# A two-layer encoder trunk on one core: constants kept across stages, loads moved into the delta mixer, three input sets and a divided softmax division in the window attention

## The reference

```
h = x * (1 + scale) + shift                      # scale, shift, gate from a conditioning vector
x = layer_norm(alpha * x + (1 + gate) * sublayer(h))
```

```
ya = (group_norm(y_fwd + y_bwd) * gn_g + gn_b + bonus * v) * (sigmoid(z_g) @ g_up)
yb = o * rsqrt(mean(o * o) + eps) * norm_g * silu(out_gate)
mixed = concat(ya, yb) @ ab_w_out
```

```
s = q @ k.T * scale + band;  m = max(max(s), sink);  p = exp(s - m)
p = p / (sum(p) + exp(sink - m));  out = p @ v
```

## Time and profile before

| what | value |
|---|---|
| median of three runs | 3577.85 us (3577.48 to 3582.41) |
| the profiled execution, its own time | 3570.47 us |
| its span (first to last instruction) | 3568.6 us |
| TensorE busy (PE) | 3123.8 us, 88% of the span |
| VectorE busy (DVE) | 1954.1 us, 55% |
| ScalarE busy (ACT) | 1243.9 us, 35% |
| GpSimd busy (POOL) | 592.1 us, 17% |
| mean granted TensorE clock | 0.912 of full speed |

### The profile page before, as it was taken

One profiled execution on the slowest core, in us unless ns is written; L12 is line 12 of the kernel. 1 busy time (PEld: TensorE's weight loads), 2 busy tenths in 40 slices (PEclk: granted clock), 3 DMA queues, 4 the chain that ended last, 5 costly groups with the idle time before them and its releaser, 6 DMA issues. The chain is left out here.

```text
span 3568.6 us, 43985 instructions
## 1 busy us (share of the span) xinstructions
PE 3123.8 (88%) x15824; PEld 1899.2 (53%) x15824; DVE 1954.1 (55%) x4102; ACT 1243.9 (35%) x2994; POOL 592.1 (17%) x547
## 2 busy tenths in 40 slices
PE   8999999679999996995895999969967889699994
PEld 4555555357777785885454444434433445444441
DVE  3886685399889873995776000045445534500016
ACT  1112222245455543673662222222245623122213
POOL 0000100111111101121000110011057810010005
PEclk9999999779788876998896999989989999699997
DMA  8453234511111002243533999943224332499986
GB/s 268 160 177 131 63 100 140 189 33 39 39 39 36 29 28 79 87 151 115 165 129 114 361 406 377 364 146 132 80 90 139 118 124 101 148 391 367 368 302 219
DMA packets 360906, 584.04 MB, mean 164 GB/s; under 512 B 50374, under 2 KB 255846, under 8 KB 360458
## 3 DMA queue, kind: packets, MB, share of 16 engines
q1 hardware_dynamic: 287624, 346.99, 29.3%
q0 software_dynamic: 34560, 123.47, 9.7%
q10 hardware_dynamic: 38532, 111.10, 8.0%
HBM read 456.81 MB, written 124.68 MB: 163 GB/s over the span
## 5 line engine op out<-in xcount | busy, mean ns | idle before, releaser
L364 PE MATMUL inp__bank<-inp__hT,inp__w 128*128 128x512 f32 (+1 forms) x1536 | 557.9, 522 | 1.0 <-DVE inp__hT L508 1.0
L2697 PE MATMUL moe__bank<-kept__weights,moe__xT 128*128 128x512 f32 x1024 | 456.8, 599 | 10.9 <-DMA kept__weights<-in_moe_w_up_dram 6.6
L364 PEld LDWEIGHTS inp__bank<-inp__hT,inp__w 128*128 128x128 f32 x1536 | 288.6, 190 | 253.2 <-issue 239.2
L2697 PEld LDWEIGHTS moe__bank<-kept__weights,moe__xT 128*128 128x128 f32 x1024 | 191.0, 192 | 234.3 <-issue 232.5
L2143 PE MATMUL close__bank<-kept__weights,kept__catT 128*128 128x512 f32 x640 | 286.5, 602 | 18.7 <-ACT kept__catT L2248 7.5
L2815 DVE TENSOR_TENSOR moe__hid<-moe__sg,moe__bank 128x256 f32<-128x256 f32 x64 | 26.9, 421 | 478.6 <-ACT moe__sg L2758 478.6
L2714 PE MATMUL moe__bank<-moe__wdn,moe__hidT 128*128 128x512 f32 x512 | 230.5, 593 | 2.9 <-ACT moe__hidT L2762 2.9
L3491 POOL TENSOR_SCALAR attn__p<-attn__p,attn__rec 128x384 f32<-128x384 f32 x160 | 195.8, 1246 | 116.7 <-DVE attn__rec L3466 116.6
L3112 PE MATMUL cq__bank<-kept__w_in,cq__hT 128*128 128x512 f32 x480 | 211.0, 596 | 2.9 <-DVE cq__hT L3248 2.9
L2143 PEld LDWEIGHTS close__bank<-kept__weights,kept__catT 128*128 128x128 f32 x640 | 121.5, 194 | 165.5 <-issue 147.0
L433 ACT ACTIVATE inp__z<-inp__bank 128x512 f32<-128x512 f32 (+1 forms) x96 | 50.5, 526 | 403.1 <-PE inp__bank L364 403.1
(11 more groups left out here) (468 smaller groups left out, 5792.3 us busy)
## 6 DMA issues: line engine op xcount, KB each, us to landing
kept__weights<-in_moe_w_gate_dram SPq DMA_DIRECT2D x64, 1024.0 KB, 8.0
kept__weights<-in_moe_w_up_dram SPq DMA_DIRECT2D x64, 1024.0 KB, 14.7
moe__wdn<-in_moe_w_down_dram ACTq DMA_DIRECT2D x64, 1024.0 KB, 8.0
inp__wv<-in_ada_w_dram SPq DMA_DIRECT2D x10, 4096.0 KB, 16.0
scratch_y_rows<-moe__y ACTq DMA_DIRECT2D x64, 512.0 KB, 8.5
scratch_zt<-inp__tb SPq DMA_DIRECT2D x32, 640.0 KB, 5.0
inp__w<-in_ab_w_in_dram POOLq DMA_DIRECT2D x31, 512.0 KB, 4.8
rwkv__rk<-scratch_zt SPq DMA_DIRECT2D x20, 512.0 KB, 3.9
```

The source lines that it names most:

```text
L364: mm = pe.matmul(zbank[j][g][:, 0:n], w[:, j, k, :], hT[:, k, t0:t0 + n], start=k == 0, stop=k == KC - 1)
L2697: mm = pe.matmul(bank[2 + j][:], xT[:, j, k, :], wgu[:, j, k].rearrange("p a n -> p (a n)"), start=k == 0, stop=k == KC - 1)
```

## The change

One copy of the first 629 constant columns, the router's three tensors and the sink row is kept in SBUF from the delta mixer on; the phases behind it no longer load their own. In `const_f`, `unit` and `eye4` move behind the masks, so that `delta` loads 704 columns (352 KB) beside the kept copy (314.5 KB). SP issues the closing part's loads inside the delta mixer's loop: five after the store of step 3, two in each of steps 4 to 6. In `close0` the first wait is for four loads in place of six, and `v`, `og` and `gn` are waited for in `joined`. In the last stage there are four sets of diagonals, three built at the start, the others ahead of each tile's squares. In the attention there are three input sets, loaded two tiles ahead, and the second head's division of every odd pair goes from GpSimd to VectorE: 40 of 160.

```diff
@@ constants
-                  ("unit", 256), ("eye4", 16)] + [
+                  ] + [
...
+        ... + [("unit", 256), ("eye4", 16), ("incl", P), ...
@@ deltanet_mixer
-        first = CONST["ident"].start
+        first = CONST["unit"].start
@@ sync
                 sp.dma_start(cf[:], a["const_f"][:, first:CONST_W]).then_inc(cst, 16)
-                sp.dma_start(ones[:], a["const_f"][:, CONST["ones"]]).then_inc(cst, 16)
+                sp.dma_start(a["cf"][:], a["const_f"][:, 0:CONST["ident"].stop]).then_inc(a["cf_l"], 16)
...
+                def closing_consts():      # gup, ng (cst_l); rw, rb, tok (router_l): five loads
...
+                def closing_heads(i):      # bon, glow of tile i (heads_l[i]): two loads
...
                     if have(s):
                         store_o(s)
+                    if s == 3:
+                        closing_consts()
+                    if 3 < s < 7:
+                        closing_heads(s - 4)
@@ close_mixer, sync
-                if layer:
-                    sp.dma_start(cf[:], a["const_f"][:, 0:CONST["ident"].stop]).then_inc(cst, 16)
...
-                        sp.dma_start(v[:, r], ...).then_inc(heads_l[r], 16)
-                        sp.dma_start(og[:, r], ...).then_inc(heads_l[r], 16)
-                        sp.dma_start(glow[:, r], ...).then_inc(heads_l[r], 16)
+                        if i > 2:          # bon and glow
...
+                        sp.dma_start(v[:, r], ...).then_inc(late_l[r], 16)
+                        sp.dma_start(og[:, r], ...).then_inc(late_l[r], 16)
...
-                sp.dma_start(rw[:], ...)   # and rb, tok
@@ close_mixer, vector
-                    dve.wait_ge(heads_l[r], 96 * (i // 3) + 96)
+                    dve.wait_ge(heads_l[r], 64 * (i // 3) + 64)
...
+                    dve.wait_ge(late_l[r], 32 * (i // 3) + 32)
+                    if i == 0:
+                        dve.wait_ge(gn_l, 32)
@@ experts, gpsimd
-                        pool.dma_start(a["ident"][:], a["const_f"][:, CONST["ident"]]).then_inc(a["cols_l"], 16)
+                        pool.dma_start(a["sink"][:], a["at_sink"].broadcast_to([P, AT_H])).then_inc(a["cols_l"], 16)
@@ combine, scalar
-                diagonals(0)
-                diagonals(1)
+                for i in range(3):
+                    diagonals(i)
                 for i in range(NT):
+                    if i + 3 < NT:
+                        diagonals(i + 3)
                     squares(i)
                     norm_rows(i)
-                    if i + 2 < NT:
-                        diagonals(i + 2)
@@ window_attention
-        v = ph.sb("v", [P, 2, 3, VW])
+        v = ph.sb("v", [P, 3, 3, VW])      # qT, kT and band alike
...
+        def on_vector(t, e):
+            return e == 1 and t % 2 == 1
...
                 load(0)
-                sp.dma_start(sink[:], a["at_sink"].broadcast_to([P, AT_H])).then_inc(cst, 16)
-                sp.dma_start(ident[:], a["const_f"][:, CONST["ident"]]).then_inc(cst, 16)
                 load(1)
+                load(2)
...
-                    if 0 < i < TILES - 1:
-                        load(i + 1)
+                    if 0 < i < TILES - 2:
+                        load(i + 2)
@@ vector
+                def divided(t):
+                    dve.wait_ge(rec_r, t + 1)
+                    h = (2 * t + 1) % AT_H
+                    dve.tensor_scalar(p[:, (2 * t + 1) % 8, 0:W3], p[:, (2 * t + 1) % 8, 0:W3], rec[:, h:h + 1], None, ALU.mult).then_inc(p_dve, 1)
...
                     if have(s_ - 1):
                         inverse(s_ - 1)
+                    if have(s_ - 1) and on_vector(s_ - 1, 1):
+                        divided(s_ - 1)
                     if have(s_ - LAG):
                         copied(s_ - LAG)
@@ gpsimd
-                        pool.tensor_scalar(...).then_inc(p_r, 1)
+                        if not on_vector(t, e):
+                            pool.tensor_scalar(...).then_inc(p_pool, 1)
```

More of the change, by code:

```diff
@@ L750, in rwkv_mixer @@
     zt, zf, y_out, bonus_out = a["zt"], a["zf"], a["rw_y"], a["rw_bonus"]
-    C0, C1 = CONST["ident"].start, CONST["mask_k1"].stop
+    C0, C1 = CONST["ident"].start, CONST["eye4"].stop
     NT = 2 * TILES
@@ L1420, in const @@
         def const(name):
-            return ones[:] if name == "ones" else cf[:, CONST[name].start - first:CONST[name].stop - first]
+            return a["cf"][:, CONST[name]] if name in ("ones", "ident") else cf[:, CONST[name].start - first:CONST[name].stop - first]
         ident = const("ident")
@@ L2028, in close_mixer @@
             yo = ph.sb("yo", [P, 3, 2, 2, RW_W])
-            bon = ph.sb("bon", [P, 3, 2, RW_H])
             v = ph.sb("v", [P, 3, RW_W])
             og = ph.sb("og", [P, 3, GD_W])
-            glow = ph.sb("glow", [P, 3, P])
-            gup = ph.sb("gup", [P, RW_W])
             gn = ph.sb("gn", [P, 2, RW_W])
-            ng = ph.sb("ng", [P, 1])
+            bon, glow, gup, ng = (a[n] for n in ("bon", "glow", "gup", "ng"))
             yn = ph.sb("yn", [P, 2, RW_W])
@@ L2680, in _ @@
             def _(pe):
-                pe.wait_ge(cst, 16)
                 pe.sem_inc(x_tr, 2)
@@ L3019, in combine_project @@
     with Phase(nc, "cq") as ph:
-        ident, w, scol, grow, ln, x, rope = (a[n] for n in ("ident", "w_in", "scol", "grow", "ln", "x_first", "rope"))
+        w, scol, grow, ln, x, rope = (a[n] for n in ("w_in", "scol", "grow", "ln", "x_first", "rope"))
+        ident = a["cf"][:, CONST["ident"]]
         y = ph.sb("y", [P, 2, 2, D])
@@ L3103, in turn_x @@
                     for k in range(KC):
-                        mm = pe.transpose(bank[k // 4][:, (k % 4) * P:(k % 4 + 1) * P], out[:, j, k * P:(k + 1) * P], ident[:])
+                        mm = pe.transpose(bank[k // 4][:, (k % 4) * P:(k % 4 + 1) * P], out[:, j, k * P:(k + 1) * P], ident)
                     mm.then_inc(x_tr, 1)
@@ L3518, in trunk @@
             a[name] = kept.sb(name, shape, dt)
+        a["cf"] = kept.sb("consts", [P, CONST["ident"].stop])
+        a["rw"], a["rb"], a["tok"] = kept.sb("rw", [P, KC, E]), kept.sb("rb", [P, E]), kept.sb("tok", [P, TILES])
+        a["sink"] = kept.sb("sink", [P, AT_H])
         big = kept.sb("weights", [P, KC * D])
@@ L3521, in trunk @@
         a["wgu"] = big[:].rearrange("p (j k a n) -> p j k a n", j=2, k=KC, a=2)
+        a["cf_l"], a["cst_l"], a["router_l"] = (kept.sem(n) for n in ("consts_loaded", "gate_weights_loaded", "router_loaded"))
+        a["heads_l"] = [kept.sem(f"heads_loaded{j}") for j in range(3)]
         a["w_out_l"] = [kept.sem(f"w_out_loaded{m}") for m in range(DEPTH)]
@@ L3529, in trunk @@
         a["x_l"] = [[kept.sem(f"x_loaded{m}{j}") for j in range(3)] for m in range(DEPTH)]
-        deltanet_mixer(nc, a)
         with ExitStack() as own:
+            for name, shape in (("ng", [P, 1]), ("bon", [P, 3, 2, RW_H]), ("gup", [P, RW_W]), ("glow", [P, 3, P])):
+                a[name] = own.enter_context(nc.sbuf_tensor(f"kept__{name}0", shape, F32))
+            deltanet_mixer(nc, a)
             a["catT"] = own.enter_context(nc.sbuf_tensor("kept__catT0", [P, 2, KC, P], F32))
```

149 lines of the change are left out of this document (76 added, 73 removed).

## The result

The changed kernel takes 3558.35 us, the median of six runs, against 3577.81 for the kernel before: a ratio of 0.9946, with a 95% interval of 0.9930 to 0.9962. It is faster, and the time lies inside the range that was given; but 19.5 us were gained where 29.8 were forecast.

The account below looks back on a forecast made before the run. TensorE, busy 88% of the span, was taken as the bound, so only its standstills could give time; in attention, a loop across TensorE, VectorE and ScalarE, not GpSimd. Terms summed to -29.8: median 3577.85 to 3548 us, range 3530 to 3570.

Parts of the forecast that it names:

- Three sets, -21: Attention: loads issued a whole tile earlier remove the scores' stall for `v`, -21 us, bounds -16 and -23.
- Its rival, that half the stalls stay: Attention: 1 MB transfers and tile loads still meet, half the stall stays, 3559 us; chance 0.09.
- Every fourth division, +6 against -3.3 at the ends: Attention: VectorE's second division waits for GpSimd, +6 us; first tile gains 2.1, last tile's drain 1.2.
- Rival (1): Attention: GpSimd keeps the port, second division waits 1.8 us, +28 instead of +6, 3570 us; chance 0.13.
- rival (2): Attention: both divisions of each half lose to GpSimd by 1.2 us and more, +48, 3590 us; chance 0.04.
- Rival (3): Attention: GpSimd is the pace after all, tiles fall to 19.3 us, -26 in all, 3519 us; chance 0.09.
- Delta mixer, -2.0: Delta mixer's start: TensorE's first product waits less because 650 KB less constants load, -2.0 us, bounds -0.5 and -2.5.
- First closing part, -5.5: Its start: VectorE's first join no longer waits for `glow`, next for `yo`; -5.5 us, bounds -4 and -6.5.
- Attention, start, -1.2: Attention's first scores no longer wait for `ident`, next for `v`; -1.2 us, bounds 0 and -1.5.
- Expert parts, 0: Expert stages: identity wait goes, but TensorE waits for gathered rows; `sink` load replaces `ident` load on GpSimd's queue; 0.
- Second closing part, -0.8: Its start: VectorE's columns still hold it, only the removed load's issue and transfer count; -0.8 us, bounds -0.4 and -3.
- Last stage, -2.0: Last stage: four diagonal sets, issued first, remove three VectorE waits behind ScalarE's norm; -2.0 us, bounds 0 and -3.

Follow-up runs that it names:

- a_two_copies: a_rows_first plus a second copy of the two moved constants at their old place for the RWKV stage: 3534.61 us, 0.9879 of before.
- a_rows_first: Changed kernel, weights tile aligned, all divisions on GpSimd, second closing part's first VectorE products taken before the columns, gate-row loads adjacent: 3537.03 us, 0.9891 of before.

## Why the prediction held, and why it was ten microseconds off

- **Three sets, -21:** right, -22.3 alone. Its rival, that half the stalls stay, had no case.
- **Every fourth division, +6 against -3.3 at the ends:** right in sign, +1.5 in all. The second division took 0.76 us, where 0.36 plus a wait of 0.6 stood, and a half tile is only 0.13 longer, not 0.3. The slack was reckoned to ScalarE's last copy; the copy that most often releases the values product is VectorE's, right behind the division. Rival (1), GpSimd keeping the port for 1.8 us, and rival (2) with it, would need divisions of 1.5 us or more; the longest is 0.757. Rival (3) would need tiles near 19.3. The first tile gained 0.65, not 2.1. The reader of the earlier trace rows should have asked what else paces that tile.
- **Delta mixer, -2.0:** -1.9.
- **First closing part, -5.5:** -4.1. The next load was `yo`, as said, but it needed 7.2 us to land in place of the 6.4 of the earlier trace rows; I had it arrive earlier.
- **Attention, start, -1.2:** -0.3, near the end of its bounds. `v` was next, and it took 8.3 us to land instead of the 6.9 of the earlier trace rows. That more sets in the queue, on which the bound rested, are the reason is not shown: with the third set alone on the kernel before `v` took 7.1 us, and in the changed kernel with two sets 7.9.
- **Expert parts, 0:** the waits ahead of their first products fell from 10.52 to 8.54 and from 9.68 to 8.23 us, -3.4. Why the gathered rows come earlier was not tested.
- **Second closing part, -0.8:** the wait ahead of TensorE's first product fell by 2.2, and the stage grew by 4.8, to 220.31: +2.5. The step "VectorE can't take the first product before its columns" was right, and the run with the gate rows first shows its price: 10 us earlier on VectorE, 7 us off the stage. But the step "Only the issue and transfer of the removed load count" failed: VectorE's first product came 24.5 us after the attention's last instead of 23.7. From there to TensorE's last product it took 1.7 us more than before, and why is open.
- **Last stage, -2.0:** about -0.9, from VectorE's first product to its last (60.4 to 59.5 us). The line that answers to the earlier trace rows shows 12.7 us in four waits. The start is 10.7 of them, as in the earlier trace rows, and tile 0's second wait 1.1; of the 2.0 us that the diagonals were to take away, 1.0 is left, in two waits:

```profile
  PE comb__bank L2922: 12.7, 4
```

- **What was left out, and the step that failed:** "The `sink` load takes the place ... 0" and every other term asked which instructions the kept tensors add or remove. None asked where the tensors behind them come to lie. That cost 8.8 + 3.3 us in the profile, and with the tile back at a multiple of 256 the kernel is at 0.9908, 28.5 us below before, close to the sum of the prediction. That closeness is partly luck: the gains of the expert parts' starts, which the sum put at 0, and the loss in the second closing part cancel. It is luck, too, that the time fell inside the range, which was wide enough for a loss that no term and no rival has. The remaining 4.6 us of the RWKV stage have no cause that these runs show.

The lowest median is that of a_two_copies, with three sets, all divisions on GpSimd, the tile aligned, the gate rows first and the second copy: 3534.61 us, 0.9879 of before. How much of its distance to a_rows_first (3537.03) is the RWKV stage's open variation can't be told.

## What to carry to other kernels

When a change keeps new tensors, write down where each streamed tile behind them begins before and after, and pad it back: here 32 bytes of padding were worth as much as all the loads that were saved. Read a stage's pace from what releases its products, not from the engine that is busiest in it. Compare the lengths of the stages that a change does not touch, over several profiles, before a gain or a loss is put down to an edit, and try the theory on one more kernel that should not move. A profile shows one execution: look where its time lies among those of its kernel.

## What the runs showed of the hardware

With the tile of the 1 MB loads 64 or 224 bytes past a multiple of 256, the first expert stage moved 352 to 355 GB/s, with it at a multiple 360 to 363, and the DMA engines were 0.97 to 0.99 busy in both; a 1 KB packet took 49.8 to 50.1 ns and 47.4 to 47.9. The Trainium skill (DMA: Bandwidth & Descriptors, "How a descriptor splits into AXI transactions") says that a transfer is cut into pieces of 256 bytes that must start at multiples of 256, so that a 1 KB piece of memory that does not start at one takes one more; it tells it of reads, and here it is the written side that was moved. Counted in such pieces 64 bytes past are as bad as 224, and the runs show no great difference (393.2 and 391.4 us). No run shows that the pieces are the cause.

A wide VectorE scale takes 0.42 us where GpSimd is idle and up to 0.757 where it is in the middle of an operation, and a GpSimd operation that begins just behind it takes 1.47 us instead of 1.24: whoever is first delays the other. The Trainium skill (SBUF — State Buffer, "Who interferes with whom") says that whoever issues first blocks the other for its whole instruction; here each lost less than the rest of the other's instruction, VectorE 0.34 us of some 0.55 and GpSimd 0.23 of 0.36. The one-column scale of the earlier trace rows is not delayed.
